# The forget term of the scores and three rows of inverse roots a layer, made without TensorE products

## What is computed

```python
def rms(x):
    xf = x.astype(jnp.float32)
    return (xf * lax.rsqrt(jnp.mean(xf * xf, axis=-1, keepdims=True) + EPS)).astype(x.dtype)
...
    log_f = jax.nn.log_sigmoid(fb.astype(f32) + b_forget.astype(f32))
    cum_f = jnp.cumsum(log_f, axis=1)
    cum_f_k = jnp.transpose(cum_f, (0, 2, 1))
...
        s_b = (jnp.einsum('bqhd,bkhd->bhqk', qb_b, kb).astype(f32) * D_B ** -0.5
               + jnp.transpose(fq_b, (0, 2, 1))[..., None] - cum_f_k[:, :, None, :])
        p_b = jax.nn.softmax(jnp.where(frame_ok, s_b, NEG_INF), axis=-1)
...
        x = x + rmsnorm(y, g[1])
        mem_n = rmsnorm(mem, mem_norm[i])
        h = rmsnorm(x, g[2])
        x = x + rmsnorm(memory_xattn(h, mem_n, wq_x[i], wkv_x[i], wo_x[i]), g[3])
```

## Time and profile before

| | us |
|---|---|
| median of 3 runs | 1987.86 (1987.84 to 1988.25) |
| span of the profiled execution, first to last instruction | 1985.5 |
| difference of the median to that span (launch and end; the profile gives no time of its own for it) | 2.4 |
| TensorE busy | 1973.6 |
| weight loads of TensorE busy (beside its products) | 1696.9 |
| VectorE busy | 1368.4 |
| ScalarE busy | 1091.7 |
| GpSimd busy | 174.4 |

### The profile page before, as it was taken

One profiled execution on the slowest core, in us unless ns is written; L12 is line 12 of the kernel. 1 busy time (PEld: TensorE's weight loads), 2 busy tenths in 40 slices (PEclk: granted clock), 3 DMA queues, 4 the chain that ended last, 5 costly groups with the idle time before them and its releaser, 6 DMA issues.

```text
span 1985.5 us, 30652 instructions
## 1 busy us (share of the span) xinstructions
PE 1973.6 (99%) x10751; PEld 1696.9 (85%) x10751; DVE 1368.4 (69%) x2102; ACT 1091.7 (55%) x1708; POOL 174.4 (9%) x199
## 2 busy tenths in 40 slices
PE   9999999999999999999999999999999999999998
PEld 8888888888888888888888888888888888888886
DVE  7957676857777777744576567768587777777445
ACT  7755466656555555444476654555665555554443
POOL 0000000001121222100000000000011221211000
PEclk9999999999999999999999999999999999999999
DMA  8564566545555555565546444665445555556552
GB/s 318 197 187 148 170 216 239 193 153 170 176 197 190 187 184 189 198 213 194 182 149 209 147 160 149 226 206 194 149 164 196 191 187 177 195 191 212 193 196 100
DMA packets 105279, 371.87 MB, mean 187 GB/s; under 512 B 12192, under 2 KB 13600, under 8 KB 103840
## 3 DMA queue, kind: packets, MB, share of 16 engines
q1 hardware_dynamic: 102176, 355.78, 53.0%
q10 hardware_dynamic: 2432, 13.23, 1.8%
q0 software_dynamic: 576, 1.57, 0.3%
HBM read 367.65 MB, written 2.88 MB: 187 GB/s over the span
## 4 chain that ended last, share of the span: by engine, by line
PE 98%; DVE 1%; issue 0%; ACT 0%; DMA 0%; DVEq 0%
PE ps L874 24%; PE ps L788 14%; PE ps L790 14%; PE ps L789 14%; PE ps L877 12%; PE ps L800 11%; PE ps L803 5%; PE ps L752 1%; PE ps L1140 1%; PE ps L1125 0%; PE ps L1128 0%; PE ps L1164 0%; PE ps L1152 0%; PE ps L1153 0%; PE ps L1151 0%; PE ps L1055 0%
## 5 line engine op out<-in xcount | busy, mean ns | idle before, releaser
L1596 DVE TENSOR_TENSOR w_lo<-raw,w_hi 128x1024 fp32r<-128x1024 f32 (+3 forms) x684 | 809.3, 1189 | 497.5 <-ACT w_hi L1209 494.5
L1209 ACT ACTIVATE w_hi<-raw 128x1024 fp32r<-128x1024 f32 (+3 forms) x684 | 700.4, 1030 | 500.9 <-PE ps L790 235.0
L874 PE MATMUL ps<-h_t,w_hi 128*128 128x512 f32 x2032 | 638.8, 396 | 0.0
L877 PEld LDWEIGHTS ps<-h_t,w_lo 128*128 128x128 f32 x2032 | 381.7, 188 | 90.2
L877 PE MATMUL ps<-h_t,w_lo 128*128 128x256 f32 x2032 | 399.2, 278 | 0.0
L874 PEld LDWEIGHTS ps<-h_t,w_hi 128*128 128x128 f32 x2032 | 309.3, 189 | 0.0
L800 PE MATMUL ps<-h_t,w_hi 128*128 128x512 f32 x768 | 244.9, 400 | 0.0
L788 PE MATMUL ps<-w_hi,act_t 128*128 128x512 f32 x512 | 199.2, 389 | 0.0
L789 PE MATMUL ps<-w_lo,act_t 128*128 128x512 f32 x512 | 199.2, 389 | 0.0
L790 PE MATMUL ps<-w_hi,act_t 128*128 128x512 f32 x512 | 199.2, 389 | 0.0
L803 PEld LDWEIGHTS ps<-h_t,w_lo 128*128 128x128 f32 x768 | 144.2, 188 | 33.9
(11 more groups left out here) (332 smaller groups left out, 2291.2 us busy)
## 6 DMA issues: line engine op xcount, KB each, us to landing
raw<-stream SPq DMA_DIRECT2D x640, 512.0 KB, 4.1
raw<-stream SPq DMA_DIRECT2D x24, 288.0 KB, 3.3
raw<-stream SPq DMA_DIRECT2D x16, 262.0 KB, 3.6
gain_a<-gains_in ACTq DMA_DIRECT2D x4, 1024.0 KB, 6.5
m_x<-mem_t_in ACTq DMA_DIRECT2D x2, 2048.0 KB, 10.2
x<-x_in SPq DMA_DIRECT2D x4, 512.0 KB, 13.2
m_nat<-mem_in ACTq DMA_DIRECT2D x1, 2048.0 KB, 11.1
gain_f<-gains_in ACTq DMA_DIRECT2D x2, 1024.0 KB, 7.8
```

Of the source, the lines that this page charges most:

```text
L874: pe.matmul(ps[:, 4 * half + nt, :], hi[:, cc, nt * P:(nt + 1) * P], h_t[:, c, :, :], start=(c == 0), stop=False, skip_group_check=True)
L877: mm = pe.matmul(ps[:, 4 * half + nt, SEQ:2 * SEQ], lo[:, cc, nt * P:(nt + 1) * P], h_t[:, c, 0, :], start=False, stop=(c == KC - 1), skip ...
L1209: act.activation(w_hi[:, slot, 0:width], raw[:, rslot, 0:width], ACT.Copy).then_inc(hi_ready, 1)
L1596: dve.tensor_tensor(w_lo[:, slot, 0:width], raw[:, rslot, 0:width], w_hi[:, slot, 0:width].bitcast(F32), ALU.subtract).then_inc(lo_ready, 1)
```

## The change

The rank products L1126 are left out. VectorE's scan stores the sums `f_row`, GpSimd sends six of its rows to HBM and fetches them twice: `f_k`, the row of sums of every head on all partitions, and `f_q`, the sum at each query as a scalar per partition. For each B head VectorE first makes `f_k` minus `f_q` plus the mask in the tile `s_sb`, with one instruction for each query block, and then adds the scaled product to it. The summed log gates change sign, so that this difference is the reference's term.

The steps R of h1, mem and h2 are left out; h3 stays. GpSimd writes the two columns to a row in HBM and fetches the row to all partitions (`factor_row`). The memory row of the second layer is fetched from the same place without being written again. VectorE waits for the fetch ahead of the first read-out that uses the row.

```diff
--- before.py
+++ after.py
@@ -194,7 +194,6 @@
     at(8 if layer else 26, ("lam",))
-    at(11 if layer else 14, ("R", "h1"))
     if layer == 0:
@@ -251,7 +250,6 @@
         at(P_OUT + 20, ("mem_rstd",))
-    at(P_OUT + 22, ("R", "mem"))
     at(P_OUT + 23, ("evac", G_OUT + 2))
@@ -262,7 +260,6 @@
     at(P_MEMK + 6, ("x_rstd", 1))
-    at(P_WQ + 1, ("R", "h2"))
     at(P_WQ + 3, ("evac", G_WQ))
@@ -418,9 +415,7 @@
         lf_ones = sb("lf_ones", [P, SEQ], BIG + 15 * K)
-        f_row = sb("f_row", [P, SEQ], BIG + 16 * K)
-        f_hi = sb("f_hi", [P, SEQ], BIG + 26 * K, F32R)
-        f_part = sb("f_part", [P, SEQ], BIG + 27 * K)
+        f_row = sb("f_row", [P, SEQ], 188 * K)
@@ -453,8 +448,8 @@
         p_t = sb("p_t", [P, 384], SCR + 4 * K + 512)
-        fa = sb("fa", [P, SEQ], SCR + 6 * K, F32R)
-        fb = sb("fb", [P, H_B, SEQ], SCR + 7 * K, F32R)
+        f_q = sb("f_q", [P, H_B, TB], SCR + 6 * K)
+        f_k = sb("f_k", [P, H_B, SEQ], SCR + 7 * K)
         t_lo = sb("t_lo", [P, 2, SEQ], SCR + 13 * K)
@@ -581,7 +576,12 @@
         lf_ready = sem("lf_ready")
-        fab_ready = sem("fab_ready")
+        f_summed = sem("f_summed")
+        f_put = sem("f_put")
+        f_got = sem("f_got")
+        r_put = sem("r_put")
+        r_got = sem("r_got")
+        rm_got = sem("rm_got")
         s_ready = sem("s_ready")
@@ -682,6 +682,8 @@
         bias_hbm0 = nc.dram_tensor("bias_hbm0", (4 * H_A, 4, 8 * P), F32, kind="Internal").ap()
+        f_hbm = nc.dram_tensor("f_hbm", (DEPTH, H_B, SEQ), F32, kind="Internal").ap()
+        r_hbm = nc.dram_tensor("r_hbm", (2 * DEPTH + 1, SEQ), F32, kind="Internal").ap()
         bias_hbm1 = nc.dram_tensor("bias_hbm1", (4 * H_A, 4, 8 * SEQ), F32, kind="Internal").ap()
@@ -1036,14 +1038,10 @@
-                        if step[1] == "mem":
-                            pe.wait_ge(rstm_ready, 1)
-                        else:
-                            pe.wait_ge(rstx_ready, l * 3 + int(step[1][1]))
-                        src = rst_m if step[1] == "mem" else rst_x
+                        pe.wait_ge(rstx_ready, l * 3 + 3)
                         b = take_bank(step)
                         for tb in range(TB):
-                            mm = pe.matmul(b[:, tb * P:(tb + 1) * P], src[:, tb:tb + 1].to_broadcast([P, P]), ident[:],
+                            mm = pe.matmul(b[:, tb * P:(tb + 1) * P], rst_x[:, tb:tb + 1].to_broadcast([P, P]), ident[:],
                                            start=True, stop=True)
@@ -1109,7 +1107,6 @@
                             pe.wait_ge(*acc_read(l, GROUP[f"kb{h // 2}"]))
-                            pe.wait_ge(fab_ready, l + 1)
                         else:
@@ -1122,8 +1119,7 @@
-                                    pe.matmul(dst, qb_t[:, h, q], kb_t[:, h, 0:nk], start=True, stop=False)
-                                    mm = pe.matmul(dst, fa[:, q], fb[:, h, 0:nk], start=False, stop=True)
+                                    mm = pe.matmul(dst, qb_t[:, h, q], kb_t[:, h, 0:nk], start=True, stop=True)
                                 else:
@@ -1454,7 +1450,7 @@
                         b = read_bank(step)
-                        free_bank(act.activation((rm_t if step[1] == "mem" else r_t)[:], b[:, 0:SEQ], ACT.Copy), step)
+                        free_bank(act.activation(r_t[:], b[:, 0:SEQ], ACT.Copy), step)
                     elif kind == "osq":
@@ -1865,12 +1861,12 @@
                                 if gi == G_MEMK:
-                                    dve.wait_ge(*item_read(l, ("R", "mem")))
+                                    dve.wait_ge(rm_got, 16 * (l + 1))
                                 k = gi - G_MEMK
...
                                 if gi == G_WQ:
-                                    dve.wait_ge(*item_read(l, ("R", "h2")))
+                                    dve.wait_ge(r_got, 16 * (2 * l + 2))
                                 k = gi - G_WQ
@@ -1879,7 +1875,7 @@
                             if name == "qb0":
-                                dve.wait_ge(*item_read(l, ("R", "h1")))
+                                dve.wait_ge(r_got, 16 * (2 * l + 1))
                             t, i = {"qa": qa_t, "ka": ka_t, "qb": qb_t, "kb": kb_t}[name[:2]], int(name[2])
@@ -2003,26 +1999,16 @@
                         for tb in range(TB):
-                            ins = dve.tensor_tensor(z_w[:, tb, :, 0:H_B], z_f[:, tb:tb + 1, :].to_broadcast(wide),
-                                                    e_f[:, tb:tb + 1, :].to_broadcast(wide), ALU.subtract)
+                            ins = dve.tensor_tensor(z_w[:, tb, :, 0:H_B], e_f[:, tb:tb + 1, :].to_broadcast(wide),
+                                                    z_f[:, tb:tb + 1, :].to_broadcast(wide), ALU.subtract)
                         ins.then_inc(lf_ready, 1)
...
                         st.done(dve.memset(lf_ones[:], 1.0))
-                        ins = dve.tensor_tensor_scan(f_row[:], lf_ones[:], b[:, 0:SEQ], 0.0, ALU.mult, ALU.add)
-                        free_bank(ins, step)
+                        free_bank(dve.tensor_tensor_scan(f_row[:], lf_ones[:], b[:, 0:SEQ], 0.0, ALU.mult, ALU.add), step)
                         dve.wait_ge(*item_read(l, step))
-                        fc = [consts[:, c:c + 1] for c in (C_FSGN, C_FSUB, C_FLO, C_FA, C_FONE)]
-                        st.done(dve.tensor_scalar(f_row[:], f_row[:], fc[0], None, ALU.mult))
-                        st.done(dve.tensor_copy(f_hi[:], f_row[:]))
-                        st.done(dve.tensor_scalar(f_part[:], f_hi[:].bitcast(F32), fc[1], None, ALU.mult))
-                        st.done(dve.scalar_tensor_tensor(f_part[:], f_row[:], fc[2], f_part[:], ALU.mult, ALU.add))
-                        dve.tensor_scalar(fa[:], f_part[:], fc[3], fc[4], ALU.mult, ALU.add)
-                        for h in range(H_B):
-                            ins = dve.tensor_scalar(fb[:, h, :], f_part[:], consts[:, C_FNEG + h:C_FNEG + h + 1],
-                                                    consts[:, C_FPOS + h:C_FPOS + h + 1], ALU.mult, ALU.add)
-                        ins.then_inc(fab_ready, 1)
+                        dve.sem_inc(f_summed, 1)
                     elif kind == "S":
@@ -2034,12 +2020,19 @@
                             j = JOB[job]
-                            b = read_bank(("S", job))
                             if j >= 3:
...
                             s = s_sb[:, j % 3, :]
+                            if hk == "B":
+                                dve.wait_ge(f_got, 32 * (l + 1))
+                                for tb, (o, nk) in enumerate(((0, P), (P, SEQ))):
+                                    ins = dve.scalar_tensor_tensor(s[:, o:o + nk], f_k[:, h, 0:nk], f_q[:, h, tb:tb + 1],
+                                                                   mask_b[:, o:o + nk], ALU.subtract, ALU.add)
+                                st.done(ins)
+                                tile = s
+                            b = read_bank(("S", job))
                             ins = dve.scalar_tensor_tensor(s, b[:, 0:384], float(scale), tile, ALU.mult, ALU.add)
@@ -2199,6 +2192,34 @@
+                def factor_row(n, src, dst, here):
...
+                    pool.dma_start(r_hbm[n].rearrange("(t p) -> p t", p=P), src[:], allow_slow_non_contiguous=True).then_inc(r_put, 16)
+                    pool.wait_ge(r_put, 16 * (n + 1))
+                    pool.dma_start(dst[:], r_hbm[n].partition_broadcast(P)).then_inc(here, 16)
...
+                pool.wait_ge(rstx_ready, l * 3 + 1)
+                if l > 0:
+                    pool.wait_ge(up_free[0], l * (UPG // 2) + 1)
+                    pool.wait_ge(up_free[1], l * (UPG // 2) + 1)
+                factor_row(3 * l, rst_x, r_t, r_got)
+                pool.wait_ge(f_summed, l + 1)
+                pool.dma_start(f_hbm[l], f_row[0:H_B, :]).then_inc(f_put, 16)
+                pool.wait_ge(f_put, 16 * (l + 1))
+                pool.dma_start(f_k[:].rearrange("p h s -> p (h s)"),
+                               f_hbm[l].rearrange("h s -> (h s)").partition_broadcast(P)).then_inc(f_got, 16)
+                pool.dma_start(f_q[:], f_hbm[l].rearrange("h (t p) -> p h t", p=P), allow_slow_non_contiguous=True).then_inc(f_got, 16)
...
+                pool.wait_ge(*item_done(l, ("O", HEADS - 1)))
+                if l == 0:
+                    pool.wait_ge(rstm_ready, 1)
+                    factor_row(1, rst_m, rm_t, rm_got)
+                else:
+                    pool.dma_start(rm_t[:], r_hbm[1].partition_broadcast(P)).then_inc(rm_got, 16)
+                pool.wait_ge(rstx_ready, l * 3 + 2)
+                pool.wait_ge(*acc_read(l, GROUP["ka1"]))
+                factor_row(3 * l + 2 if l == 0 else 4, rst_x, r_t, r_got)
```

## The result

The changed kernel takes **1993.03 us** (median of 7 runs, 1989.02 to 1994.03) against 1987.96 us for the kernel before on the same chip (7 runs, 1987.84 to 1988.25): a ratio of 1.0023, 95% interval 1.0014 to 1.0032. It is slower by about 0.2%, where 1982.4 us was forecast, and outside the range. The profiled execution took 1991.44 us, its span is 1989.6 us.

The account below looks back on a forecast made before the run. TensorE was taken to bound the kernel; from the 1987.86 us median, 2.64 us (forget term) and 2.78 us (rows) were subtracted, all else counted as nothing, giving 1982.4 us. The range reached from 0.2 us below 1981.7 up to 1986.5 us.

Parts of the forecast that it names:

- What bounds the kernel: TensorE, 98% of the chain of waits; each product removed shortens the run if nothing behind it comes late.
- Forget term: Leaving out the L1126 products of six B heads in two layers saves TensorE 12 x 0.22 = 2.64 us.
- Rows: Leaving out the h1, mem and h2 products (L1046) saves TensorE 2 x (0.45 + 0.45 + 0.49) = 2.78 us.
- VectorE's added work: Two instructions per B head, 10 us in all, cost TensorE nothing; as rival, half shows, 1987.4 us, chance 0.06.
- The forget rows, the first and the memory's row: Their round trips through HBM on GpSimd's queue arrive before they are wanted and cost nothing.
- The query's chain: From query inverse roots through HBM to VectorE: 9.4 us, between 5.2 and 19.9; VectorE waits 1.4 us a layer, TensorE none.
- The tolerance: The query's row may come 12.4 us after its inverse roots before TensorE waits for a weight split.
- the late row: Query factor late at first qx read-out, both layers: beyond 12.4 us each us costs two, up to 1997.4 us; chance 0.09.
- The estimate from a page: The skill's fit, 2.0 us plus bytes at 436 GB/s, gives the query's transfers 4.3 us, so VectorE would not wait.
- GpSimd's descriptors: Rival: in the h2 stretch descriptors wait for VectorE's splits, chain 14.3 us, 1.9 us late a layer, 1986.2 us; chance 0.05.
- the products were not free: Against the rival that removed TensorE products only filled time while the next weights load: 1987.9 us, chance 0.04.

Follow-up runs that it names:

- the run with the bystander: The kernel before plus one unused GpSimd write a layer of the query's inverse roots to HBM as 256 single elements: 1987.77 us, ratio 1.0001.

## Why the prediction was wrong

- **What bounds the kernel: right.** TensorE's busy time fell by 4.6 us in the version with the later read-out, which has no gap for the row (1969.0 us), and every gain or loss appeared at its starts.
- **Forget term: right, a little small.** 0.22 us a head was taken, 12 x 0.256 = 3.07 us measured; the upper end of 0.27 us, for a main product that also gets faster, was nearer. The difference between median and span, taken as fixed at 2.4 us, fell by 0.3 to 0.4 us with it (2.2 to 1.8 us on average). The chain now shows a B head's tile at 0.66 us, as forecast: "157.09 0.66 PE ps L1122 x4".
- **Rows: 2.78 us counted, 1.65 to 1.7 measured.** The first and the memory's row bring 0.83 of 0.90 us a layer. The query's brings nothing. The step that failed is the condition "as long as nothing behind it (a weight piece, a factor, a probability tile) comes later than TensorE now asks for it": without the product the next pair starts 0.38 us late, for the split behind the inverse roots, and takes 0.10 us longer. I priced the product by its place in the chain and did not ask what VectorE was doing under it.
- **VectorE's added work: right.** Two rows a head of 339 and 480 ns, the exponential of the second B head done at 168.65 us, its transposes at 171.04 us, so 2.4 us to spare (2.6 forecast), and no wait for it:

```profile
L2031 DVE SCALAR_TENSOR_TENSOR s_sb<-f_k,f_q,mask_b x24: 339/409/480, 157.1 to 1205.0; 128x128 f32<-128x128 f32 x12, 128x256 f32<-128x256 f32 x12
```

- **The forget rows, the first and the memory's row: right.** None is waited for, though the writes of the first and the memory's row take about 9 us as well, and the first stops the stream for 8 us at 116 to 124 us (0 and 35 GB/s). The writes of the forget rows, six rows of 1 KB, take 6.5 us in layer 0 and 2.8 us in layer 1.
- **The query's chain: the step that failed most.** "I take 9.4" was 15.9 and 16.8 us. The tolerance was nearly right, 12.4 us against 13.0. The nearest rows were the bias writes, which leave in long runs, and the write in question has 256 single elements: 8.6 and 8.9 us against the 3.6 taken. The prediction said that no row priced this, and then took the row of the other kind. The read was taken at 4.7 us and measured 6.6 and 7.3. Here the trace before had the price. The row of inputs stands for two transfers, and its 4.7 us is only the middle between one of 6.6 us, issued at 21.8 us where the core moved 392 GB/s, and one of 2.8 us, issued at 1012.2 us where it moved 209. Between two ends of 5.2 and 19.9 us with a tolerance of 12.4 us in the middle, a chance of 0.09 for the late row was far too small. The two transfers of the inputs in the kernel before (tile `rows`):

```profile
DMA to landing us min/median/max: 2.8/4.7/6.6
```

- **The estimate from a page.** The Trainium skill's fit on the page "DMA: Bandwidth & Descriptors", section "Anatomy of one DMA — SWDGE (gpsimd) path", gave an estimate of 4.3 us for the chain. The runs say 15.9 and 16.8 us with single elements; for the write in two pieces it is near (2.0 us by the fit, 1.5 measured), for the 128 KB read beside the stream it is not (2.3 us by the fit, 3.8 and 3.2 us in that run, 6.6 and 7.3 in the kernel after). The Trainium skill's warning of a strided last dimension, in "Rules for kernel authors" of the page "DMA: Bandwidth & Descriptors", is what the runs bear out: 8.6 to 8.9 us with 256 single elements, 4.1 to 4.3 us with half as many pieces.
- **The late row as a rival: right in its place and form.** By its own formula a chain of 16.35 us gives 1982.4 + 2 x (16.35 - 12.4) = 1990.3 us; measured 1993.0. Lacking are the query's row at its full price (1.0 us too much gained) and the low clock, against which stand the larger tolerance and forget term. With these at their measured sizes (1.0 us for the query's row, 0.1 for the other rows and 1.6 for the clock more; 1.2 for the tolerance and 0.8 for the forget term less) the formula gives 1991.0 us, and the profiled execution took 1991.4.
- **The clock: no term at all.** Its price is 1.6 us behind one gap, and with the gaps filled the runs lie within 1.7 us where they lay within 5.0.
- **The other rivals.** GpSimd's descriptors do not wait for VectorE (the issue takes 0.71 us beside a running split, and the leg is as long from ScalarE's queue); VectorE's added work does not show (no wait for the B heads' tiles); the products were not free, but the query's row was.

## What to carry to other kernels

A column that is written to HBM element by element is priced by how it is cut up and not by its bytes alone: the same 1 KB took 8.8 us, in half as many pieces 4.3 us, in two 1.5 us, and the other transfers nearly stood still under the single elements. When the nearest row is the middle of two or three transfers, look at each of them, and take the one with the same traffic beside it. Where a wait is added to an engine's queue, look at what is queued behind it and how long that can stand: the same row, as late as it was, cost 5 us or nothing by the place of its reader. Before you credit a removed product, see whether a slower engine was finishing something beneath it.

## What had not been expected of the hardware

- A write of 256 single four-byte elements from 128 partitions to HBM takes 8.5 to 10.0 us from either queue, and in the 4 us stretches under it all traffic is down to between 0 and 53 GB/s; then it catches up, at over 400 GB/s in the run with the bystander. Why the others stop is not shown. It is not so for a read of single elements: f_q, 1,536 of them, lands after 8.0 us, and in the 4 us stretches beside it the kernel after moves 231 and 216 GB/s.

```profile
136.00:140.00 4.00, 4.00 (x29) 3.64 (x28) 3.29 (x5) 2.73 (x8) 0.00 (x0) 1.00 0.78 231
140.00:144.00 4.00, 4.00 (x24) 3.51 (x24) 1.96 (x6) 2.38 (x7) 0.00 (x0) 1.00 0.62 216
```

- The granted clock fell behind gaps of TensorE of 2.07, 2.08, 2.43, 2.70, 3.33, 3.52 and 3.77 us, and did not behind gaps of 2.60 and 2.93 us (the write from ScalarE's queue) and 2.84 us (layer 0 of the kernel after). In these traces the length of a gap alone does not decide it. With the gap filled by transposes it stayed at 1.00.
